# A fused two-block transformer layer on one core: down products two tiles behind, normed sums through PSUM, casts at other places, and the third FFN's RMS factor applied to its gate and up tiles

## What is computed

```
first block:  x = layer_norm(a*x + 0.5 * swiglu_0(x))        FFN 0, d_ff = 2816
              x = layer_norm(a*x + mixer(x))                  qkv of three kinds of attention, gates, w_out
              x = layer_norm(a*x + 0.5 * swiglu_1(x))        FFN 1
second block: u = rmsnorm(h, g_pre);  h = h + rmsnorm(mix(u), g_post)
              f = rmsnorm(h, ffn_pre) @ w_up                  FFN 2, "the third FFN"
              f = causal_dwconv(f, width 3) + bias;  gate, val = split(f)
              f = (gelu(gate) * val) @ w_down;  h = h + rmsnorm(f, ffn_post)
              e = (p @ w_ple) * sigmoid(h @ w_ple_gate);  h = h + rmsnorm(e, ple_post)
rmsnorm(x, w) = x * rsqrt(mean(x^2) + 1e-6) * w        one factor per token, one gain per feature
```

## Time and profile before

| | |
|---|---|
| time, median of 3 runs | 1193.85 us (1192.21 to 1196.79) |
| the profiled execution | 1193.65 us |
| its span, first to last instruction | 1191.8 us |
| mean granted TensorE clock | 0.976 of full speed |
| PE busy | 1114.9 us, 94% of the span |
| POOL busy | 908.9 us, 76% |
| ACT busy | 628.6 us, 53% |
| DVE busy | 516.9 us, 43% |

### The profile page before, as it was taken

How to read it: one execution, slowest core, us unless ns; L and a number is a source line. 1 busy time by engine, 2 the same in 40 slices (tenths; PEclk the granted TensorE clock), 3 DMA queues, 4 the chain that set the end, 5 groups by cost and what they waited for, 6 DMA issues and landing times.

```text
span 1191.8 us, 22559 instructions
## 1 busy us (share of the span) xinstructions
PE 1114.9 (94%) x8040; PEld 1034.4 (87%) x8040; DVE 516.9 (43%) x979; ACT 628.6 (53%) x1012; POOL 908.9 (76%) x700
## 2 busy tenths in 40 slices
PE   6999998899999998899998899899899989999986
PEld 6999998898988897799998889899788879999964
DVE  3333116232336544511113547774665245455664
ACT  4444446555556755344444765554556575555553
POOL 7999995998553595999998599393225869999973
PEclk9999999999998999999999899999989999999988
DMA  7866664576331364566565366252213655666641
GB/s 253 323 203 199 194 192 127 175 207 189 112 114 54 107 200 160 171 194 191 188 194 186 106 201 188 89 159 72 71 54 118 192 159 178 193 190 187 196 151 53
DMA packets 52631, 193.40 MB, mean 162 GB/s; under 512 B 5840, under 2 KB 6096, under 8 KB 51920
## 3 DMA queue, kind: packets, MB, share of 16 engines
q1 hardware_dynamic: 50976, 184.57, 49.8%
q10 hardware_dynamic: 1584, 7.81, 1.8%
HBM read 191.31 MB, written 1.05 MB: 161 GB/s over the span
## 4 chain that ended last, share of the span: by engine, by line
POOL 51%; issue 31%; PE 14%; DVE 2%; POOLq 1%; ACT 1%; DVEq 0%; ACTq 0%
POOL weights_low L498 51%; PE banks L529 8%; PE acc L529 6%; POOLq L501 0%; DVE xs L1797 0%; POOLq L495 0%; DVE stat L1812 0%; DVE res L1810 0%; DVE res L1824 0%; DVE act_buf L1672 0%; DVE xs L1830 0%; DVE xs L1793 0%; ACT weights_high L1165 0%; DVE hf L1680 0%; ACT act_buf L1208 0%
## 5 line engine op out<-in xcount | busy, mean ns | idle before, releaser
L498 POOL TENSOR_TENSOR weights_low<-ring,weights_high 128x512 fp32r<-128x512 f32 x696 | 908.7, 1336 | 263.9 <-ACT weights_high L1165 260.7
L1165 ACT CAST weights_high<-ring 128x1024 fp32r<-128x1024 f32 x348 | 361.5, 1048 | 242.8 <-PE banks L529 123.7
L529 PE MATMUL banks<-xT_high,weights_high 128*128 128x256 f32 x1536 | 432.0, 281 | 3.3 <-POOL weights_low L498 2.8
L529 PE MATMUL banks<-xT_low,weights_high 128*128 128x256 f32 x1536 | 427.4, 278 | 0.0
L529 PE MATMUL banks<-xT_high,weights_low 128*128 128x256 f32 x1536 | 427.2, 278 | 0.0
L529 PEld LDWEIGHTS banks<-xT_high,weights_high 128*128 128x128 f32 x1536 | 290.7, 189 | 7.2 <-issue 3.0
L529 PEld LDWEIGHTS banks<-xT_low,weights_high 128*128 128x128 f32 x1536 | 290.9, 189 | 2.3
L529 PEld LDWEIGHTS banks<-xT_high,weights_low 128*128 128x128 f32 x1536 | 290.3, 189 | 0.0
L1647 DVE TENSOR_TENSOR hf<-act_buf,banks 128x256 f32<-128x256 f32 x40 | 16.9, 421 | 247.4 <-ACT act_buf L1191 247.3
L529 PE MATMUL acc<-weights_high,hT_high 128*128 128x512 f32 x264 | 103.6, 392 | 7.6 <-issue 6.7
L529 PE MATMUL acc<-weights_low,hT_high 128*128 128x512 f32 x264 | 104.0, 394 | 0.0
(11 more groups left out here) (337 smaller groups left out, 1620.6 us busy)
## 6 DMA issues: line engine op xcount, KB each, us to landing
ring<-in_stream SPq DMA_DIRECT2D x348, 512.0 KB, 3.6
rows<-in_big_rows ACTq DMA_DIRECT2D x3, 1024.0 KB, 6.9
rows<-in_big_rows ACTq DMA_DIRECT2D x3, 512.0 KB, 4.4
cst<-in_consts ACTq DMA_DIRECT2D x1, 1411.0 KB, 10.8
gates<-in_x_fm SPq DMA_DIRECT2D x2, 512.0 KB, 5.2
xs<-in_x_tm ACTq DMA_DIRECT2D x1, 1024.0 KB, 6.0
out<-xs SPq DMA_DIRECT2D x4, 256.0 KB, 2.1
pT<-in_p_fm ACTq DMA_DIRECT2D x1, 256.0 KB, 3.5
```

The source lines that it names most:

```text
L498: last = nc.gpsimd.tensor_tensor(wlo[:, slot, hs], ring[:, slot, hs], whi[:, slot, hs].bitcast(F32), ALU.subtract)
L529: ins = nc.tensor.matmul(o, lhsT, rhs, start=start, stop=stop, **kw)
L1165: nc.scalar.copy(whi[:, ch % RING, :], ring[:, ch % RING, :]).then_inc(S["hi_ready"], 1)
```

## The change

1. **Down products two tiles behind.** The order becomes gate_up(2), gate_up(3), down(0), down(1), gate_up(4), down(2), and then gate_up(f), down(f-2). The stream is packed in that order, and `ffn_end` counts the feed accordingly.
2. **Sums through PSUM.** `add_normed` writes the product with the gain back to `acc`, and the second instruction reads `acc` in place of `xs`. The semaphores that it raises go on after the sum.
3. **Casts.** `turn` on ACT casts the fourth chunk of the following stage between its second and third group. Ahead of turn(3) the copies of `ple` stand ahead of `x_rms`, with a cast ahead of each pair. Ahead of turn(4) no cast stands between the squares of the two token halves; two stand behind both.
4. **The third FFN's factor.** `rms_scaled` is gone. turn(3) turns the unscaled sum `xs[:, 0]`. `x_rms` stands behind the turn on ACT. DVE spreads each token's factor over a 128x128 tile (`rb`), PE turns it behind gate_up_first, DVE copies it to `row_r` (one row of 256 token factors on every partition), and `conv_hidden` multiplies each tile of 128x512 by it in PSUM before ACT reads it. ACT waits for `scaled` in place of `job_done`.

```diff
 def ffn_end(f):
-    return 32 if f < 2 else 24 * f + (8 if f < NF - 1 else 0)
+    return 32 if f < 2 else 16 * f + 16 if f < 4 else 24 * f
...
@@ PE
+        rb, row_r = xc[:, 0], bdv[:, 0, :]
...
                 gate_up_first()
+                if n == 2:
+                    pe.wait_ge(S["rb_ready"], 1)
+                    for tok in range(2):
+                        last = nc.tensor.matmul(acc[:, 3, P * tok:P * tok + P], rb[:, tok, 0:P], ident, start=True, stop=True)
+                    last.then_inc(S["row_scale"], 1)
                 gate_up(2)
+                gate_up(3)
                 down(0)
                 down(1)
-                for f in range(3, 1 + GROUP):
-                    gate_up(f)
-                    down(f - 1)
+                gate_up(4)
+                down(2)
                 with nc.tensor.Fori(1, (NF - 2) // GROUP - 1) as it:
                     for f in range(1, 1 + GROUP):
                         gate_up(f + GROUP, it - 1)
-                        down(f - 1 + GROUP, it - 1)
+                        down(f - 2 + GROUP, it - 1)
                 for f in range(NF - 1 - GROUP, NF - 1):
                     gate_up(f)
-                    if f < NF - 2:
-                        down(f - 1)
+                    down(f - 2)
                 gate_up(NF - 1)
...
-            turn(3)
+            turn(3, xs[:, 0])
             ffn(2)
             turn(4, xs[:, 1])
@@ ACT, geglu_act
-                act.wait_ge(S["job_done"], j + 1 + GROUP * it)
+                act.wait_ge(S["scaled"], f + 1 + GROUP * it)
...
-            def turn(i, gain=None, bias=None):
+            def turn(i, following, gain=None, bias=None):
                 for g in range(4):
+                    if g == 2:
+                        feed_to(PART_AT[following] // CB + 4)
                     job_wait(act, f"turn{i}.{g}")
...
             acc_rms(12, 0)
-            feed_to(PART_AT["ple"] // CB + 3)
+            feed_to(PART_AT["ple"] // CB + 2)
             acc_rms(12, 1)
+            for k in range(4):
+                if k % 2 == 0:
+                    feed_to(PART_AT["ffn2"] // CB + 1 + k // 2)
+                ple_copy(k)
+            feed_to(PART_AT["ffn2"] // CB + 3)
+            turn(3, "ffn2", "ffn_pre")
             x_rms(4, 0, 0)
-            ple_copy(0)
-            ple_copy(1)
             x_rms(4, 0, 1)
-            ple_copy(2)
-            ple_copy(3)
-            feed_to(PART_AT["ffn2"] // CB + 3)
-            turn(3, "ffn_pre")
             rows_in(5)
             over_ffn(2, geglu_act)
             warm(ACT.Sqrt)
             acc_rms(16, 0)
-            feed_to(PART_AT["ple_gate"] // CB + 1)
             acc_rms(16, 1)
-            feed_to(PART_AT["ple_gate"] // CB + 3)
-            turn(4)
+            feed_to(PART_AT["ple_gate"] // CB + 2)
+            turn(4, "ple_gate")
@@ DVE, conv_hidden
+                dve.wait_ge(S["job_done"], index["ffn2.0"] + f + 1 + GROUP * it)
+                tile = ffn_tile(2, f, it).rearrange("p (a t) -> p a t", a=2)
+                v.tensor_tensor(tile, tile, row_r.unsqueeze(1).broadcast_to([P, 2, T]), ALU.mult).then_inc(S["scaled"], 1)
                 dve.wait_ge(S["tap_in"], f + 1 + GROUP * it)
@@ DVE, add_normed
-                        mark(v.tensor_tensor(xs[:, dst, tok, hs], acc[:, 2 * tok + half, :], rows[:, i % 2, hs], ALU.mult),
-                             "acc_read", (12, 16)[i - 3] + 2 * tok + half + 1)
+                        link(v.tensor_tensor(acc[:, 2 * tok + half, :], acc[:, 2 * tok + half, :], rows[:, i % 2, hs], ALU.mult))
                     link(recip(stds + tok + 1, tok))
                     for half, (_, hs) in enumerate(halves(tok)):
-                        v.scalar_tensor_tensor(xs[:, dst, tok, hs], xs[:, dst, tok, hs], stat[:, 6 + tok:7 + tok], xs[:, src, tok, hs],
-                                               ALU.mult, ALU.add).then_inc(S[sem], 1)
+                        mark(v.scalar_tensor_tensor(xs[:, dst, tok, hs], acc[:, 2 * tok + half, :], stat[:, 6 + tok:7 + tok],
+                                                    xs[:, src, tok, hs], ALU.mult, ALU.add), sem, sem0 + 2 * tok + half + 1)
@@ DVE, program
-            rms_scaled(0, 10 + 1, 0)
-            rms_scaled(0, 10 + 2, 1)
             turn(3, "ffn_pre")
+            for tok in range(2):
+                link(recip(10 + tok + 1, tok))
+                last = v.tensor_copy(rb[:, tok, 0:P], stat[:, 6 + tok:7 + tok].broadcast_to([P, P]))
+            last.then_inc(S["rb_ready"], 1)
+            dve.wait_ge(S["row_scale"], 1)
+            mark(v.tensor_copy(row_r, acc[:, 3, 0:T]), "row_scaled", 1)
             over_ffn(conv_hidden)
```

More of the change, by code:

```diff
@@ L597, in project_tm, with into_acc @@
                             done(last)
-            def into_acc(src, each, first_wait):
+            def into_acc(src, each, free):
                 (high, high0), (low, low0) = each
@@ L604, in into_acc @@
                     if k == 0:
-                        pe.wait_ge(S["acc_read"], first_wait)
+                        pe.wait_ge(S[free[0]], free[1])
                     w = [weights(4), weights(4)]
@@ L907, in _ @@
                 branch_b(n)
[L908 removed]
+            into_acc(mT1, (("merged_high", 0), ("merged", 0)), ("acc_read", 4))
             turn(1)
@@ L1319, in _ @@
             feed_to(PART_AT["qk"] // CB + 3)
-            turn(0, "ln_g0", "ln_b0")
+            turn(0, "qk", "ln_g0", "ln_b0")
             scale = {0: 0.125, 2: float(np.float32(32 ** -0.5)), 4: 0.125}
@@ L1392, in _ @@
             feed_to(PART_AT["ffn1"] // CB + 3)
-            turn(1, "ln_g1", "ln_b1")
+            turn(1, "ffn1", "ln_g1", "ln_b1")
             rows_in(2)
@@ L1450, in _ @@
             feed_to(PART_AT["conv"] // CB + 3)
-            turn(2, "mix_pre")
+            turn(2, "conv", "mix_pre")
             def conv_silu(t):
@@ L2286, in ffn_blocks @@
     g, u, d = (a.reshape(NF, 8, P, P) for a in (fm_blocks(gate), fm_blocks(up), tm_blocks(down)))
-    parts = [by_k(np.concatenate([g[0], u[0], g[1], u[1]]), 4), g[2], u[2], d[0], d[1]]
-    for f in range(3, NF):
-        parts += [g[f], u[f]] + ([d[f - 1]] if f < NF - 2 else [])
+    parts = [by_k(np.concatenate([g[0], u[0], g[1], u[1]]), 4), g[2], u[2], g[3], u[3], d[0], d[1]]
+    for f in range(4, NF):
+        parts += [g[f], u[f]] + ([d[f - 2]] if f < NF - 1 else [])
     return parts + [d[NF - 3], d[NF - 2], d[NF - 1]]
```

33 lines of the change are left out of this document (15 added, 18 removed).

## The result

The changed kernel takes 1189.55 us (median of 15 runs, 1185.23 to 1198.82), beside it the kernel before 1196.19 us (15 runs, 1190.79 to 1201.85): ratio 0.9946, 95% interval 0.9923 to 0.9969. That is 6.5 us less (3.7 to 9.2), at the edge of what can be told from no change. The spans of the two profiled executions differ by 4.0 us: 1187.8 us in place of 1191.8.

The account below looks back on a forecast made before the run. PE, busy 94% of the span, was taken to bound the kernel, so gains come only where it waits or runs at half clock. -1.3 - 5.4 + 0.6 + 5.1 - 3.0 = -4.0 us off 1193.85 gave 1189.7 us, range 1183.5 to 1197.

Parts of the forecast that it names:

- the forecast case: Whole kernel: the sum of all terms, 1189.7 us, range 1186 to 1193, chance 0.45.
- Turn casts, 1.3 us: qk stage: fourth chunk cast earlier, 1.3 us gained of 2.83 lost there (bounds 0 and 2.8).
- removes the 1.47 us: FFN 1: the fourth chunk, cast about 3 us earlier, ends PE's 1.47 us wait for it.
- FFN 1, 5.4 us: FFN 1: wait ahead of first down product, half clock and fourth chunk's wait go, less new waits: 5.4 us gained.
- both new waits: FFN 1: chunks 8 and 9, made by POOL beside `layer_out`, come late; PE waits 1.0 and 1.3 us.
- turn(3) and the head of FFN 2, 4.2 gained and 4.8 lost: 4.2 us earlier by gate_up_first's end, 4.8 lost behind it, with PE waiting 5.6 us for chunk 7 in gate_up(3).
- The loop, 5.1 us: FFN 2's loop: the row-factor multiplication delays Gelu and cast, 5.1 us lost (bounds 1.1 and 14).
- 0.32 us in each of the loop's 16 tiles: Loop: multiplication shifts the chunk by 0.74 us, 0.42 late, about 0.1 saved; 0.32 us lost in every tile.
- turn(4), 3.0 us: turn(4): shorter sums and a moved cast start its last group 2.5 us earlier, plus 0.5 of clock: 3.0 us gained.
- Case 2: Loop: row factor hidden, 0.07 us lost a tile; FFN 2's head gains 1 us; 1184 us, chance 0.27.
- Case 3: Loop: DVE becomes the ring, 8.6 us above 8.21, next multiplication starts late; slower, 1199.8 us at 0.95 a tile; chance 0.09.
- Case 4: FFN 1: wait ahead of `down(0)` only moves to chunks 7 to 9; gain 1.5 for 5.4, 1193.6 us, chance 0.19.

## Why the prediction came out

The time, 1189.7 us, was met by 1189.55, and the forecast case was the one that ran. That it was met to 0.15 us is luck in three ways. The forecast took 4.0 us off 1193.85, a median of three executions; beside the changed kernel the kernel before has 1196.19, so the measured difference is 6.5 us (3.7 to 9.2). The profiled difference is 4.0 us, as in the sum, but 1.9 us of it come from the second mixer, in which I predicted nothing and which scatters by 6.7 us between traces; without it the change made 2.1 us in this pair. And the terms were off on both sides: the gains of FFN 1 and turn(4) were taken too large, and so was the loop's loss.

- **Turn casts, 1.3 us:** 1.4 in the pair, 1.5 over all traces. What failed is the step "removes the 1.47 us" as the whole of the rest: the cast is worth 0.7 us in FFN 1 and 4.6 in turn(3) and gate_up_first. The latter is inside my 4.2 us for turn(3), which I put down to the squares alone. They hid the missing chunk; with them gone the cast has to be early too.
- **FFN 1, 5.4 us:** 4.1 in the pair, 5.1 over the traces with the turn casts. The mechanism held, both new waits were smaller than mine (0.23 and 0.53 us idle for 1.0 and 1.3). The half clock went at 486 us, but in this trace it lasted 6.8 us in turn(1) in place of 3.4. Four other traces with the turn casts have 3.4 us there, and FFN 1 takes 186.6 to 187.0 us in them, 5.5 to 5.9 less than before.
- **turn(3) and the head of FFN 2, 4.2 gained and 4.8 lost:** 3.6 and 5.2. Each link came within 0.2 us of its place: counted from the end of gate_up_first (963.8), tile 0's Gelu ended at 5.1 us, the multiplication at 7.0, the second Gelu at 10.3, the cast at 11.3, POOL at 13.9. PE waited 4.9 us for the 5.6 predicted, since it came there at 9.1 us and not at 8.5, and ran at half clock behind it.
- **The loop, 5.1 us:** 3.6. The multiplication took the 0.70 us taken for it, and the cast was late for the reason given, by 0.4 us rather than 0.32. The step that failed is "0.32 us in each of the loop's 16 tiles": a late chunk costs half its lateness a tile, 0.22 us here, not all of it.
- **turn(4), 3.0 us:** 2.2, the second instruction taking 0.75 us for 0.69, in place of 0.99 to 1.2 with both inputs in SBUF. The sums made about half.
- **Case 2** (row factor hidden) is out in the loop. **Case 3** did not occur in the changed kernel, but one step behind it, when POOL was fed earlier. **Case 4** is out: the wait in FFN 1 did not move on.

What stays open: why PE is at the lower clock for 13.7 us of the second mixer in one trace and for up to 27.3 in another, and why FFN 0's tiles took 8.42 us in place of 8.21 in two traces (down products two tiles behind alone, and the scalar form without the turn casts), about 3 us in all, with PE busy throughout and the granted clock at 1.00. And of the 9 us that the missing turn casts cost about 1 is not found in a stage.

## What to carry to other kernels

When an operation is put into a ring of engines, count from the event that starts a round to the instruction that waits, and ask whether the wait shifts the next start: here lateness cost half. Slack won at one place (down products two tiles behind) is only worth what is moved into it: the split behind the next multiplication and a cast into ACT's wait made 8.7 us of it, where each alone lost 3.5 and 8.6 us against the changed kernel. Before feeding an engine earlier, look at which of its neighbours ran in the pause that goes.

## What the runs showed of the hardware

A DVE operation with two inputs in SBUF and one element a partition (the difference in the qk stage) took 7.81 us before, 7.85 in the changed kernel, 7.2 to 12.3 in seven more traces, 35.46 without the turn casts and 0.44 in the run with DVE's new order alone, while POOL ran its subtractions without a pause; as a tensor_scalar it took 0.21 us in both runs that had it. In the 35.46 us POOL began 28 of its operations of 1.3 us, in the 7.81 us 6. So it looks as if such an operation can be passed over by many POOL instructions in a row, not only by the one that runs. DVE's products and subtractions of 128x256 with two inputs in SBUF never took more than 1.61 us in the FFNs of any trace, and why the small one is passed over and they are not stays open.

The copy from SBUF to SBUF (hT_high, one input) took 0.29 us beside a pausing POOL and 1.28 beside a running one, while the multiplication with one input in PSUM stayed at 0.68 to 0.70 in each run. The Trainium skill, SBUF — State Buffer, section "SBUF: two separate sides", says that the loser of the shared port pair fully blocks while the other's instruction runs, and that an fp32 copy from SBUF to SBUF runs in a mode that takes both ports. The copy's rows agree, and the 35.46 us go beyond it.
